# Routing and gather fed from the centred, weighted input, with factor and shift applied later, and token-on-partition variance sums

## The chip, the cores and the metric

One core of a Trainium2 chip runs the whole program in one launch. The metric is device time in microseconds, lower is better. TensorE is PE, VectorE is DVE, ScalarE is ACT, GpSimd is POOL, SyncE is SP.

## The reference, cut to what matters

Two transformer blocks run one after the other on x [1, 256, 1024], fp32. The second one is changed. Its two layers have a mixer (NSA, then MLA) and a mixture of 16 experts, each followed by a LayerNorm:

```python
def layer_norm(x, g, b):                 # LN_EPS = 1e-5
    mu = jnp.mean(xf, -1, keepdims=True)
    var = jnp.mean(jnp.square(xf - mu), -1, keepdims=True)
    y = (xf - mu) * lax.rsqrt(var + LN_EPS) * g + b
for i in range(2):
    ...                                  # y = mixer output @ w_out[i]
    x = layer_norm(DEEPNORM_ALPHA * x + y, ln_g[i, 0], ln_b[i, 0])
    f = hier_moe(x, ...)                 # 4 groups of 4 experts
    x = layer_norm(DEEPNORM_ALPHA * x + f, ln_g[i, 1], ln_b[i, 1])
# hier_moe: logits xs @ w_grp + b_grp (4) and xs @ w_exp + b_exp (16);
# best group, best 2 experts in it; sum of gate * (silu(x W_g) * (x W_u)) W_d
```

## The kernel before

x lies with features on partitions, as [128, 8, 256]: eight chunks of 128 features by 256 tokens. There are four LayerNorms (`LayerNorm`, L2033), numbered 0 to 3: 0 and 2 stand before the experts (the routing norms), 1 before MLA, 3 at the end. Each sums x over the features by ones times chunk on PE (L2062), centres on DVE (L2106), squares on ACT (L2083), sums the squares by ones times chunk on PE (L2068, 256 columns wide, the sum in every row), takes the square root of 128x256 on ACT (L2085) and the reciprocal on DVE (L2113), scales on DVE in four pieces (L2117), and applies gain g and shift b on ACT (L2093, six chunks) and DVE (L2121, two). `keep_busy` (its matmul is L323) issues matmuls on zeros, fillers. Norm 1 also carries `MemoryRows`: PE transposes of loaded memory rows (L2162), ACT copies of them (L2185), products (L2173).

The experts (`Moe`, L2749) start with routing. PE forms 20 logits a token from x (L2903) with a filler behind each chunk, and transposes x so that tokens lie on partitions (L2947), which ACT copies to `tok`. DVE finds the groups (from L3243), PE ranks the tokens (L2913 to L2915), DVE writes one-hot places (L3279 for slot 0, L3283 for the others), and PE gathers slot 0's tokens by them (L2960). ACT writes the rounded half x_hi (L3114), DVE the rest x_lo (L3312). Before the experts PE also transposes the one-hots (L2926), multiplies them with the gates (L2933), and each engine loads a plan (L2848), which says if a fifth slot of tokens is run.

Then run four expert groups of eight weight steps each, two a expert for gate and up, two for down. A step is 1 MB or 2 MB of weights from a ring that SP fills. ACT rounds a piece to w_hi (L3136, L3144), DVE forms w_lo (L3318, L3324), and PE does 24 matmuls of three products each step (L2964 to L2966). The order on every engine is the order in which each class's `pe`, `act` and `dve` issue; semaphores (`x_ready`, `ln_*`, `gu_hi`, `gu_lo`) and a PSUM bank plan connect them. `dve_first` (L3235) does the first weight pieces of step 0 inside the norm.

## Time and profile before

| | |
|---|---|
| Time, median of 3 runs | 2118.66 us (2119.27, 2115.07, 2118.66) |
| Profiled execution, its own time | 2114.99 us |
| Its span in the trace | 2113.2 us |
| Mean granted clock of PE | 0.996 |
| Busy share of PE, DVE, ACT, POOL | 97%, 69%, 53%, 1% |
| Weights and inputs read | 416.70 MB, 198 GB/s over the span |

PE is busy nearly all the time; the other engines have slack on average. The mean hides that in each routing stretch the engines work one after the other. These stretches are short, so they are read in the list of instructions by time, not in the shares. The granted clock is the share of the full 2.4 GHz that the chip gave PE: 1.00 is that level, 0.5 is 1.2 GHz.

### The profile page before, as it was taken

To read this page: it belongs to the slowest core of one execution; us is meant where nothing else is said; L and a number is where in the kernel's file an instruction comes from. 1 tells how busy PE (TensorE), PEld (TensorE's weight loads), DVE (VectorE), ACT (ScalarE), POOL (GpSimd) and SP (SyncE) were. 2 spreads that over 40 slices of the span, in tenths; PEclk is the share of its full clock that TensorE was granted. 3 is DMA by queue.
4 is the path that set the end of the run, shared out by engine and by line. 5 is a ranking of instruction groups with operands and counts; after the bars stand their busy time and mean duration, and the time that the engine had idled before them with its cause. 6 is when DMAs were issued, how large, how long until landed. Compare 5 with 4: busy or idle time off the path is not lost. (4 is left out here: it accounts for less than half of the span.)

```text
span 2113.2 us, 34585 instructions
## 1 busy us (share of the span) xinstructions
PE 2044.1 (97%) x14050; PEld 1853.5 (88%) x14050; DVE 1464.0 (69%) x2157; ACT 1114.7 (53%) x1580; POOL 26.3 (1%) x35
## 2 busy tenths in 40 slices
PE   7999999999999999989999989999999889999998
PEld 7999997999999998879999967888888758888886
DVE  5666785666666665576665477788987466888896
ACT  4333733544343445574333456677775455776774
POOL 1000000000000020000000000000000000000000
PEclk9999999999999999999999999999999999999999
DMA  9555322655545543435553532589985514789992
GB/s 310 186 186 184 123 89 92 211 185 186 186 148 185 185 146 100 154 124 189 186 184 124 156 123 100 204 323 368 351 328 207 220 40 160 271 328 337 343 359 93
DMA packets 246671, 421.44 MB, mean 199 GB/s; under 512 B 7716, under 2 KB 135104, under 8 KB 246432
## 3 DMA queue, kind: packets, MB, share of 16 engines
q1 hardware_dynamic: 245632, 418.09, 56.2%
q0 software_dynamic: 544, 1.62, 0.2%
q8 instruction: 73, 1.20, 0.2%
q10 hardware_dynamic: 384, 0.21, 0.1%
q14 instruction: 38, 0.31, 0.0%
HBM read 416.70 MB, written 1.05 MB: 198 GB/s over the span
## 5 line engine op out<-in xcount | busy, mean ns | idle before, releaser
L662 PE MATMUL banks<-x_hi,w_hi 128*128 128x256 f32 x1360 | 385.8, 284 | 0.0
L663 PE MATMUL banks<-x_lo,w_hi 128*128 128x256 f32 x1360 | 384.9, 283 | 0.0
L664 PE MATMUL banks<-x_hi,w_lo 128*128 128x256 f32 x1360 | 384.8, 283 | 0.0
L3318 DVE TENSOR_TENSOR w_lo<-weight_ring,w_hi 128x1024 fp32r<-128x1024 f32 x256 | 300.3, 1220 | 25.4 <-ACT w_hi L3136 16.9
L608 ACT ACTIVATE w_hi<-weight_ring 128x1024 fp32r<-128x1024 f32 x87 | 92.0, 1057 | 419.3 <-PE banks L664 419.2
L624 DVE TENSOR_TENSOR w_lo<-weight_ring,w_hi 128x1024 fp32r<-128x1024 f32 x88 | 107.7, 1224 | 242.4 <-ACT w_hi L608 242.4
L3136 ACT ACTIVATE w_hi<-weight_ring 128x1024 fp32r<-128x1024 f32 x256 | 256.0, 1053 | 36.0 <-PE banks L2966 20.4
L1084 DVE TENSOR_TENSOR pieces<-weight_ring,pieces 128x512 fp32r<-128x512 f32 (+2 forms) x245 | 167.8, 692 | 144.4 <-ACT pieces L1073 141.9
L662 PEld LDWEIGHTS banks<-x_hi,w_hi 128*128 128x128 f32 x1360 | 261.1, 192 | 0.2
L663 PEld LDWEIGHTS banks<-x_lo,w_hi 128*128 128x128 f32 x1360 | 261.1, 192 | 0.1
L664 PEld LDWEIGHTS banks<-x_hi,w_lo 128*128 128x128 f32 x1360 | 261.1, 192 | 0.0
L1018 PE MATMUL banks<-split,pieces 128*128 128x256 f32 (+2 forms) x824 | 239.6, 291 | 4.6 <-DVE split L451 2.6
L1073 ACT ACTIVATE pieces<-weight_ring 128x512 fp32r<-128x512 f32 (+2 forms) x245 | 151.9, 626 | 173.1 <-PE banks L1020 172.5
L1019 PE MATMUL banks<-split,pieces 128*128 128x256 f32 (+2 forms) x824 | 235.0, 285 | 0.0
L1020 PE MATMUL banks<-split,pieces 128*128 128x256 f32 (+2 forms) x824 | 234.8, 285 | 0.0
L615 DVE TENSOR_TENSOR w_lo<-weight_ring,w_hi 128x2048 fp32r<-128x2048 f32 x87 | 198.8, 2285 | 9.7 <-ACT w_hi L604 9.7
L2964 PE MATMUL banks<-w_hi,x_hi 128*128 128x512 f32 x512 | 202.9, 396 | 0.6 <-DVE w_lo L3318 0.6
L2966 PE MATMUL banks<-w_lo,x_hi 128*128 128x512 f32 x512 | 199.7, 390 | 0.0
L662 PE MATMUL banks<-h_hi,w_hi 128*128 128x256 f32 x704 | 199.5, 283 | 0.0
L2965 PE MATMUL banks<-w_hi,x_lo 128*128 128x512 f32 x512 | 199.3, 389 | 0.0
L663 PE MATMUL banks<-h_lo,w_hi 128*128 128x256 f32 x704 | 199.2, 283 | 0.0
L664 PE MATMUL banks<-h_hi,w_lo 128*128 128x256 f32 x704 | 199.2, 283 | 0.0
(406 smaller groups left out, 4079.8 us busy)
## 6 DMA issues: line engine op xcount, KB each, us to landing
weight_ring<-in_ffn_w_in SPq DMA_DIRECT2D x88, 1024.0 KB, 7.6
weight_ring<-in_moe_w_gate SPq DMA_DIRECT2D x64, 1024.0 KB, 6.6
weight_ring<-in_moe_w_up SPq DMA_DIRECT2D x64, 1024.0 KB, 9.0
weight_ring<-in_moe_w_down SPq DMA_DIRECT2D x48, 1024.0 KB, 11.9
weight_ring<-in_ffn_w_out SPq DMA_DIRECT2D x44, 1024.0 KB, 9.8
weight_ring<-in_moe_w_down SPq DMA_DIRECT2D x8, 2048.0 KB, 11.5
weight_ring<-in_hg_w_in SPq DMA_DIRECT2D x12, 1024.0 KB, 8.2
weight_ring<-in_fox_w_in SPq DMA_DIRECT2D x12, 1024.0 KB, 8.4
```

The source lines that it names most:

```text
L615: dve.tensor_tensor(k.w_lo[:, b, 0:2048].rearrange("p (k n) -> p k n", n=P), raw[:, 0:4096].rearrange("p (k n) -> p k n", n=256)[:, :, jj ...
L662: pe.matmul(out, w_hi, m_hi, start=start, stop=False, skip_group_check=True)
L663: pe.matmul(out, w_hi, m_lo, start=False, stop=False, skip_group_check=True)
L664: return pe.matmul(out, w_lo, m_hi, start=False, stop=stop, skip_group_check=True)
L1018: pe.matmul(out, l_hi, r_hi, start=start, stop=False, skip_group_check=True)
L1019: pe.matmul(out, l_hi, r_lo, start=False, stop=False, skip_group_check=True)
L1020: return pe.matmul(out, l_lo, r_hi, start=False, stop=stop, skip_group_check=True)
L2964: pe.matmul(out, m_hi, w_hi, start=start, stop=False, skip_group_check=True)
L2965: pe.matmul(out, m_lo, w_hi, start=False, stop=False, skip_group_check=True)
L2966: return pe.matmul(out, m_hi, w_lo, start=False, stop=stop, skip_group_check=True)
L3136: act.activation(self.gate_up_piece(s, p, self.w_hi), self.gate_up_piece(s, p), ACT.Copy).then_inc(sem["gu_hi"], 1)
L3318: dve.tensor_tensor(self.gate_up_piece(s, p, self.w_lo), self.gate_up_piece(s, p), self.gate_up_piece(s, p, self.w_hi.bitcast(F32)), ALU.s ...
```

## The change

In the routing norms, logits and transposes are taken from the centred x times g (`dve_gain`, `act_gain`). The factor 1/std is applied to the logits and in the copies to `tok`, the shift b in x_hi and x_lo (as bias), and b times the routing weights is added by eight 20-column matmuls. x itself, wanted again at the group's end, is scaled and shifted inside the first group (`dve_scale`, `act_shift`). In every norm the variance sums are matmuls of one column with the squares stationary, so std has a row for each token; where the factor is wanted along rows, a diagonal matrix times ones spreads it (`pe_rows`). In the routing norms DVE adds the first six chunks of x during the mixer (`dve_mean`). Place transposes, gates and the others' one-hots move into group 0, the plan's load into the last group. The fillers of the routing norms go, save four; the last norm has 12 for 17.

```diff
@@ -1213,6 +1215,8 @@
                 dve.wait_ge(k.x_ready, 4 * self.turn + done + 1)
                 k.banks.release(dve, f"{self.out_name}_o{done}")
+            if self.norm_after:
+                self.norm_after.dve_mean(dve, c)
@@ -2056,22 +2064,88 @@
         out = b.claim(pe, f"ln_m{i}")[:, 0:T]
+        if self.adds:
+            pe.wait_ge(k.ln_added, self.adds)
+            for kk in range(2):
+                pe.matmul(out, k.ones, k.sq[:, kk], start=kk == 0, stop=False)
+            pe.wait_ge(k.x_ready, 4 * self.before)
+            for kk in (KD - 2, KD - 1):
...
+        b.filled(last, f"ln_m{i}")
+        if self.routes is None:
+            self.sums_to = b.claim(pe, f"ln_v{i}")
+            for c in range(4):
+                last = self.pe_sums(pe, c)
+            b.filled(last, f"ln_v{i}")
+            self.pe_rows(pe)
+            if self.memory:
+                self.memory.pe_turned(pe)
+                self.memory.pe_products(pe)
+            else:
+                k.keep_busy(pe, k.psum[:, 0, :], 12)
+            return
...
-            last = pe.matmul(out, k.ones, k.x[:, kk], start=kk == 0, stop=kk == KD - 1)
...
-            last = pe.matmul(out, k.ones, k.sq[:, kk], start=kk == 0, stop=kk == KD - 1)
...
-        if not self.memory:
-            k.keep_busy(pe, k.psum[:, 0, :], 17)
...
+            last = pe.matmul(out, self.shift(kk).to_broadcast([P, P]), k.w_route[:, self.routes, kk], start=kk == 0, stop=kk == KD - 1)
+        b.filled(last, f"ln_c{i}")
+        self.sums_to = b.claim(pe, f"ln_v{i}")
+        self.logits_to = b.claim(pe, f"ln_lg{i}")
+        self.pe_sums(pe, 0)
+        self.pe_sums(pe, 1)
+        self.pe_logits(pe, 0)
+        self.pe_sums(pe, 2)
+        b.filled(self.pe_sums(pe, 3), f"ln_v{i}")
+        for c in (1, 2, 3):
+            last = self.pe_logits(pe, c)
+        b.filled(last, f"ln_lg{i}")
+    def pe_sums(self, pe, c):
+        k = self.k
+        pe.wait_ge(k.ln_sq, 4 * self.i + c + 1)
+        for kk in (2 * c, 2 * c + 1):
+            for t in range(TT):
+                last = pe.matmul(self.sums_to[:, t:t + 1], k.sq[:, kk, t * P:(t + 1) * P], k.ones[:, 0:1],
+                                 start=kk == 0 and t == 0, stop=kk == KD - 1, skip_group_check=True)
+        return last
+    def pe_logits(self, pe, c):
...
+        pe.wait_ge(k.ln_gained_dve if c < 2 else k.ln_gained_act, 2 * self.routes + c % 2 + 1)
+        for kk in (2 * c, 2 * c + 1):
+            for t in range(TT):
+                last = pe.matmul(self.logits_to[:, t * n:(t + 1) * n], k.x[:, kk, t * P:(t + 1) * P], k.w_route[:, self.routes, kk],
+                                 start=kk == 0 and t == 0, stop=kk == KD - 1, skip_group_check=True)
+        return last
+    def pe_rows(self, pe):
...
+        pe.wait_ge(k.ln_diag, 2 * self.i + 2)
+        for t in range(TT):
+            last = pe.matmul(out[:, t * P:(t + 1) * P], k.ones, self.diag[:, t * P:(t + 1) * P], start=True, stop=True, skip_group_check=True)
...
+    def act_shift(self, act, c):
...
+        act.activation(k.x[:, 2 * c], k.x[:, 2 * c], ACT.Identity, bias=self.shift(2 * c))
+        act.activation(k.x[:, 2 * c + 1], k.x[:, 2 * c + 1], ACT.Identity, bias=self.shift(2 * c + 1)).then_inc(k.x_ready, 1)
@@ -2081,17 +2155,59 @@
-        if self.memory:
-            act.wait_ge(k.x_ready, 4 * self.before)
-            self.memory.act_turned(act)
+        if self.routes is not None:
+            self.act_gain(act, 2)
+        src = b.wait(act, f"ln_v{i}")[:, 0:TT]
...
+        if self.routes is not None:
+            self.act_gain(act, 3)
+            return
         for c in range(3):
...
+        if self.memory:
+            act.wait_ge(k.x_ready, 4 * self.before)
+            self.memory.act_turned(act)
+    def act_gain(self, act, c):
...
+        act.activation(k.x[:, 2 * c], k.xn[:, 2 * c], ACT.Copy, scale=self.gain(2 * c))
+        act.activation(k.x[:, 2 * c + 1], k.xn[:, 2 * c + 1], ACT.Copy, scale=self.gain(2 * c + 1)).then_inc(k.ln_gained_act, 1)
+    def dve_gain(self, dve, c):
...
+        dve.tensor_scalar(k.x[:, 2 * c], k.xn[:, 2 * c], self.gain(2 * c), None, ALU.mult)
+        dve.tensor_scalar(k.x[:, 2 * c + 1], k.xn[:, 2 * c + 1], self.gain(2 * c + 1), None, ALU.mult).then_inc(k.ln_gained_dve, 1)
+    def dve_mean(self, dve, c):
...
+        if c == 1:
...
+            k.dve_seq.inc(dve.tensor_tensor(k.sq[:, 0:2], k.x[:, 0:2], k.x[:, 2:4], ALU.add))
...
+        if c == 2:
...
+            dve.tensor_tensor(k.sq[:, 0:2], k.sq[:, 0:2], k.x[:, 4:6], ALU.add).then_inc(k.ln_added, 1)
+            self.moe.dve_first(dve, (0,))
+    def dve_scale(self, dve, c):
...
+        dve.tensor_tensor(k.x[:, cs], k.x[:, cs], k.rstd[:].unsqueeze(1).to_broadcast([P, 2, T]), ALU.mult).then_inc(k.ln_scaled, 1)
+    def dve_rstd(self, dve):
...
+        k.banks.wait_read(dve, f"ln_v{i}")
+        dve.reciprocal(self.rstd_col, self.std_col).then_inc(k.ln_rstd, 1)
+        dve.wait_ge(k.ln_rstd, i + 1)
+        for t in range(TT):
+            dve.tensor_scalar(self.diag[:, t * P:(t + 1) * P], k.ident, self.rstd_col[:, t:t + 1], None, ALU.mult).then_inc(k.ln_diag, 1)
@@ -2107,19 +2223,26 @@
-        dve.reciprocal(k.rstd[:], k.std[:]).then_inc(k.ln_rstd, 1)
-        dve.wait_ge(k.ln_rstd, i + 1)
+        if self.routes is not None:
+            self.dve_gain(dve, 0)
+            self.dve_gain(dve, 1)
+            src, both = b.wait(dve, f"ln_c{i}")[:, 0:G_N + E_N], k.b_route[:, self.routes]
+            k.dve_seq.inc(dve.tensor_tensor(both, src, both, ALU.add))
+            k.dve_seq.wait(dve)
+            b.release(dve, f"ln_c{i}")
+            self.dve_rstd(dve)
+            return
+        self.dve_rstd(dve)
+        rstd = b.wait(dve, f"ln_r{i}")[:, 0:T].unsqueeze(1).to_broadcast([P, 2, T])
         for c in range(4):
             cs = slice(2 * c, 2 * c + 2)
-            dve.tensor_tensor(k.xn[:, cs], k.xn[:, cs], k.rstd[:].unsqueeze(1).to_broadcast([P, 2, T]), ALU.mult).then_inc(k.ln_scaled, 1)
+            dve.tensor_tensor(k.xn[:, cs], k.xn[:, cs], rstd, ALU.mult).then_inc(k.ln_scaled, 1)
...
+        b.release(dve, f"ln_r{i}")
         for kk in (KD - 2, KD - 1):
             g, bb = self.affine(kk)
             dve.tensor_scalar(k.x[:, kk], k.xn[:, kk], g, bb, ALU.mult, ALU.add).then_inc(k.ln_last, 1)
...
@@ -2894,18 +3021,11 @@
-        for kk in range(KD):
...
-                pe.wait_ge(k.x_ready, 4 * (self.turn - 1) + kk // 2 + 1)
-            for t in range(TT):
-                last = pe.matmul(out[:, t * 20:(t + 1) * 20], k.x[:, kk, t * P:(t + 1) * P], k.w_route[:, self.layer, kk],
...
-            k.keep_busy(pe, k.psum[:, 0, :], 1, 256)
-        b.filled(last, name + "lg")
...
-            self.pe_x_turned(pe, q)
+        self.pe_x_turned(pe, 0)
+        self.pe_x_turned(pe, 2)
+        self.norm.pe_rows(pe)
+        self.pe_x_turned(pe, 1)
+        self.pe_x_turned(pe, 3)
@@ -2913,30 +3033,45 @@
-        self.pe_x_turned(pe, 3)
         k.keep_busy(pe, k.psum[:, 0, :], 4, 256)
         pe.wait_ge(sem["placed"], 2 * self.layer + 2)
...
+    def pe_places(self, pe):
...
+        for i in range(self.SLOTS_N):
+            for t in range(TT):
+                last = pe.matmul(out[:, i * E_G:(i + 1) * E_G], self.place[:, t, i * P:(i + 1) * P], self.best[:, t], start=t == 0, stop=t == 1)
...
-        k.keep_busy(pe, k.psum[:, 0, :], 6)
...
-                last = pe.matmul(out[:, i * E_G:(i + 1) * E_G], self.place[:, t, i * P:(i + 1) * P], self.best[:, t], start=t == 0, stop=t == 1)
...
-        k.keep_busy(pe, k.psum[:, 0, :], 4)
-        count = self.load_plan(pe)
...
+    def act_places(self, act):
...
+        for q in range(3):
...
+            act.activation(self.place_t[:, q * 512:q * 512 + w], self.place_bank(q)[:, 0:w], ACT.Copy).then_inc(sem["places_read"], 1)
@@ -3037,6 +3172,9 @@
+            if s == 2 and i == 0:
+                self.pe_places(pe)
+                pe.wait_ge(sem["places_read"], 4 * self.layer + 4)
@@ -3085,22 +3223,20 @@
...
-            b.read(act.activation(self.tok[:, q // 2, (q % 2) * 512:(q % 2 + 1) * 512], src, ACT.Copy), f"{name}x{q}")
+            b.read(act.activation(self.tok[:, q // 2, (q % 2) * 512:(q % 2 + 1) * 512], src, ACT.Copy,
+                                  scale=self.norm.rstd_col[:, q // 2:q // 2 + 1]), f"{name}x{q}")
+            if q == 2:
+                src = b.wait(act, f"ln_r{self.norm.i}")[:, 0:T]
+                b.read(act.activation(k.rstd[:], src, ACT.Copy), f"ln_r{self.norm.i}")
...
         for c in range(2):
...
-            b.read(act.activation(self.place_t[:, q * 512:q * 512 + w], src[:, 0:w], ACT.Copy), f"{name}st{q}")
-        count = self.load_plan(act)
...
-        b.read(act.activation(self.gates[:, :, 0:E_G], src, ACT.Copy), name + "gates")
-        self.slots(act, count, self.act_slot, self.act_last_slot, self.act_skip)
+        self.slots(act, self.act_slot, self.act_last_slot, self.act_skip)
@@ -3111,8 +3247,9 @@
-        act.activation(self.x_hi[:, 4 * c:4 * c + 4], k.psum[:, 2 + c, :].rearrange("p (k n) -> p k n", n=P),
-                       ACT.Copy).then_inc(sem["xs_hi"], 1)
+        for n in range(4):
+            ins = act.activation(self.x_hi[:, 4 * c + n], k.psum[:, 2 + c, n * P:(n + 1) * P], ACT.Identity, bias=self.norm.shift(4 * c + n))
+        ins.then_inc(sem["xs_hi"], 1)
@@ -3189,7 +3326,11 @@
+                    if i == 0 and s == 2:
+                        self.act_places(act)
                 self.act_gate_up(act, s, p, self.step(i, s))
+            if i == 0 and s >= 4:
+                self.norm.act_shift(act, s - 4)
             if e:
@@ -3229,8 +3370,11 @@
-        count = self.load_plan(dve)
-        self.dve_slots(dve, count)
+        self.dve_tokens(dve, 0, 0)
+        self.dve_first(dve, (3,))
+        self.dve_tokens(dve, 0, 1)
+        self.dve_gates(dve)
+        self.dve_slots(dve)
@@ -3247,22 +3391,19 @@
...
+        lg = f"ln_lg{self.norm.i}"
+        src = b.wait(dve, lg)[:, 0:40].rearrange("p (t n) -> p t n", t=2)
+        for t in range(TT):
+            seq.inc(dve.scalar_tensor_tensor(out=self.logits[:, t], in0=src[:, t], scalar=self.norm.rstd_col[:, t:t + 1],
+                                             in1=k.b_route[:, self.layer], op0=ALU.mult, op1=ALU.add))
+        seq.wait(dve)
+        b.release(dve, lg)
@@ -3277,16 +3418,52 @@
+        do(dve.scalar_tensor_tensor(out=self.over, in0=src[0:1, 8:12], scalar=float(P), in1=k.const(C_LAST, 4, 1),
+                                    op0=ALU.is_gt, op1=ALU.mult))
+        b.release(dve, name + "rank")
+        self.dve_first(dve, (2,))
...
+    def dve_spread(self, dve):
...
         for t in range(TT):
             dve.tensor_tensor(self.place[:, t, P:6 * P].rearrange("p (i n) -> p i n", n=P),
...
+        do(dve.tensor_reduce(self.over[:, 0:1], self.over, X_AXIS, ALU.min))
+        do(dve.tensor_scalar(k.plan[:, 0:1], self.over[:, 0:1], 0.0, float(G_N), ALU.is_lt, ALU.add))
+        dve.tensor_scalar(k.plan[:, 1:2], self.over[:, 0:1], float(G_N), float(G_N - 1), ALU.add, ALU.min).then_inc(sem["planned"], 1)
+    def dve_gates(self, dve):
@@ -3299,18 +3476,15 @@
-        do(dve.tensor_reduce(self.over[:, 0:1], self.over, X_AXIS, ALU.min))
...
-        for c in range(2):
-            self.dve_tokens(dve, 0, c)
...
-                          self.x_hi[:, 4 * c:4 * c + 4].bitcast(F32), ALU.subtract).then_inc(sem["xs_lo"], 1)
+        for n in range(4):
+            ins = dve.scalar_tensor_tensor(out=self.x_lo[:, 4 * c + n], in0=k.psum[:, 2 + c, n * P:(n + 1) * P],
+                                           scalar=self.norm.shift(4 * c + n), in1=self.x_hi[:, 4 * c + n].bitcast(F32),
+                                           op0=ALU.add, op1=ALU.subtract)
+        ins.then_inc(sem["xs_lo"], 1)
     def dve_gate_up(self, dve, s, p, n):
@@ -3384,6 +3560,12 @@
+            if i == 0 and s == 1:
+                self.dve_spread(dve)
+            if i == 0 and 3 <= s < 7:
+                if s == 3:
+                    k.banks.wait_read(dve, f"ln_r{self.norm.i}")
+                self.norm.dve_scale(dve, s - 3)
```

PE, layer 0, between mean sums and routing. Before, the last variance sums and what follows (`squares`: x squared, `zeros`: filler, `x_res`: x):

```order
L2068 MATMUL banks<-squares,consts 128x256 [waits ln_sq]
L2068 MATMUL banks<-squares,consts 128x256
L323 MATMUL banks<-zeros 128x512 x17
L2903 MATMUL banks<-w_route,x_res 128x20 [waits x_ready,bank_free_0,small_ready]
L2903 MATMUL banks<-w_route,x_res 128x20
L323 MATMUL banks<-zeros 128x256
L2903 MATMUL banks<-w_route,x_res 128x20 x2
L323 MATMUL banks<-zeros 128x256
```

After, the same place:

```order
L2114 MATMUL banks<-consts,squares 128x1 [waits ln_sq,bank_free_1,bank_free_0]
L2114 MATMUL banks<-consts,squares 128x1 x3
L2114 MATMUL banks<-consts,squares 128x1 [waits ln_sq]
L2114 MATMUL banks<-consts,squares 128x1 x3
L2124 MATMUL banks<-w_route,x_res 128x20 [waits ln_gained_dve]
L2124 MATMUL banks<-w_route,x_res 128x20 x3
L2114 MATMUL banks<-consts,squares 128x1 [waits ln_sq]
```

The sums have one column, and logits stand between them without fillers.

DVE, layer 0, from the gates into the first weight steps. Before:

```order
L3302 TENSOR_REDUCE squares<-squares 1x1
L3303 TENSOR_SCALAR moe_plan<-squares 1x1 [waits dve_seq]
L3304 TENSOR_SCALAR moe_plan<-squares 1x1 [waits dve_seq]
L3312 TENSOR_TENSOR x_lo<-banks,x_hi 128x512 [waits moe_xs_hi] x2
L2848 TENSOR_LOAD moe_plan [waits moe_planned,bank_free_1]
L2848 ISA x2
L3318 TENSOR_TENSOR w_lo<-weight_ring,w_hi 128x1024 [waits moe_gu_hi] x4
L3318 TENSOR_TENSOR w_lo<-weight_ring,w_hi 128x1024 [waits moe_gu_lo,moe_gu_hi]
```

After (step 0's pieces, the other one-hots and the plan, then step 1's next pieces):

```order
L3478 TENSOR_TENSOR squares<-squares 128x8 [waits dve_seq]
L3492 TENSOR_TENSOR w_lo<-weight_ring,w_hi 128x1024 [waits moe_gu_hi] x4
L3446 TENSOR_REDUCE squares<-squares 128x2 [waits moe_gu_lo]
L3447 TENSOR_SCALAR squares<-squares 128x2 [waits dve_seq]
L3449 TENSOR_TENSOR wide<-consts,squares 128x640 [waits dve_seq]
L3449 TENSOR_TENSOR wide<-consts,squares 128x640
L3452 TENSOR_REDUCE squares<-squares 1x1
L3453 TENSOR_SCALAR moe_plan<-squares 1x1 [waits dve_seq]
L3454 TENSOR_SCALAR moe_plan<-squares 1x1 [waits dve_seq]
```

The gates and the one-hots for the other slots are now among weight pieces.

ACT in the norm before MLA. Before, from the square root on (`arena`: copies of memory rows):

```order
L2085 ACTIVATE std<-banks,consts 128x256 [waits bank_ready_3]
L2185 ACTIVATE arena<-banks 128x512 [waits bank_ready_0,x_ready]
L2185 ACTIVATE arena<-banks 128x512 [waits bank_ready_1]
L2185 ACTIVATE arena<-banks 128x512 [waits bank_ready_2]
L2185 ACTIVATE arena<-banks 128x512 [waits bank_ready_3]
L2093 ACTIVATE x_res<-wide,params 128x256 [waits ln_scaled]
```

After:

```order
L2169 ACTIVATE x_res<-wide,params 128x256
L2169 ACTIVATE x_res<-wide,params 128x256 [waits ln_scaled]
L2169 ACTIVATE x_res<-wide,params 128x256
L2308 ACTIVATE arena<-banks 128x512 [waits bank_ready_3,x_ready]
L2308 ACTIVATE arena<-banks 128x512 [waits bank_ready_0]
L2308 ACTIVATE arena<-banks 128x512 [waits bank_ready_1]
```

The memory copies now stand behind the six affine operations.

## Rows read from the trace of the kernel before

**Rows 1.** PE by time, layer 0: start, us, engine, line, tiles, shape, count [idle before].

```profile
1311.33 3.61 PE L2062 MATMUL banks<-x_res,consts 128*128 128x256 f32 x16
...
1320.00 3.83 PE L323 MATMUL banks<-zeros 128*128 128x512 bf16 x17
...
1325.01 0.52 PE L2903 MATMUL banks<-w_route,x_res 128*128 128x20 f32 x4
1325.37 0.27 PE L323 MATMUL banks<-zeros 128*128 128x256 bf16 x1
...
1327.88 0.89 PE L2903 MATMUL banks<-w_route,x_res 128*128 128x20 f32 x4
...
1328.77 2.67 PE L2947 MATMUL banks<-consts,x_res 128*128 128x128 f32 x12
...
1332.79 3.84 PE L2960 MATMUL banks<-wide 128*128 128x128 f32 x32
...
1338.85 2.29 PE L2933 MATMUL banks<-squares,wide 128*128 128x4 f32 x20
...
1341.71 0.55 PE L2964 MATMUL banks<-w_hi,x_hi 128*128 128x512 f32 x1
```

**Rows 2.** PE in order of time, layer 1.

```profile
1771.15 3.61 PE L2062 MATMUL banks<-x_res,consts 128*128 128x256 f32 x16
...
1788.15 1.47 PE L2947 MATMUL banks<-consts,x_res 128*128 128x128 f32 x12
```

**Rows 3.** ACT in order of time: the first SiLU of each expert layer.

```profile
1352.99 0.60 ACT L3150 ACTIVATE silu_gate<-banks 128x512 f32<-128x512 f32 x1 [1.66 <-PE banks L2966]
...
1811.38 0.60 ACT L3150 ACTIVATE silu_gate<-banks 128x512 f32<-128x512 f32 x1 [1.65 <-PE banks L2966]
```

**Rows 4.** busy by stretch, PE to POOL (instructions); last, granted clock and DMA share.

```profile
1324.40:1327.80 3.40, 3.34 (x35) 3.37 (x36) 1.40 (x4) 1.88 (x4) 0.00 (x0) 1.00 1.05 402
1327.80:1331.30 3.50, 3.50 (x20) 3.50 (x20) 1.82 (x11) 1.17 (x2) 0.00 (x0) 0.51 0.66 259
1357.00:1407.00 50.00, 50.00 (x236) 41.42 (x235) 44.30 (x42) 36.61 (x41) 0.00 (x0) 1.00 0.90 337
```

**Rows 5.** DVE in order of time, layer 0.

```profile
1312.36 2.36 DVE L3318 TENSOR_TENSOR w_lo<-weight_ring,w_hi 128x1024 fp32r<-128x1024 f32 x2
1314.98 2.48 DVE L2106 SCALAR_TENSOR_TENSOR wide<-banks,x_res 128x512 f32<-128x512 f32 x4 [0.26 <-PE banks L2062]
...
1320.71 1.75 DVE L2113 RECIPROCAL rstd<-std 128x256 f32<-128x256 f32 x1 [0.75 <-ACT std L2085]
1322.50 2.50 DVE L2117 TENSOR_TENSOR wide<-wide,rstd 128x512 f32<-128x512 f32 x4
1325.03 0.74 DVE L2121 TENSOR_SCALAR x_res<-wide,params 128x256 f32<-128x256 f32 x2
...
1333.04 1.56 DVE L3283 TENSOR_TENSOR wide<-consts,squares 128x640 f32<-128x640 f32 x2
...
1334.81 0.17 DVE L3252 TENSOR_TENSOR squares<-squares 128x8 f32<-128x8 f32 x1
...
1338.00 0.17 DVE L3301 TENSOR_TENSOR squares<-squares 128x8 f32<-128x8 f32 x1
```

**Rows 6.** ACT in order of time, layer 0.

```profile
1323.22 3.06 ACT L2093 ACTIVATE x_res<-wide,params 128x256 f32<-128x256 f32 x6 [2.55 <-DVE wide L2117]
...
1334.88 0.60 ACT L3114 ACTIVATE x_hi<-banks 128x512 fp32r<-128x512 f32 x1
```

**Rows 7.** ACT by form: shape, count | busy us, mean ns | idle before.

```profile
L1673 ACT ACTIVATE arena<-arena,att_cols 128x128 f32<-128x128 f32 x8 | 3.1, 386 | 0.0
```

**Rows 8.** PE and ACT in order of time, the norm before MLA.

```profile
1646.81 1.97 PE L2162 MATMUL banks<-consts,weight_ring 128*128 128x128 f32 x16 [3.39 <-DMA weight_ring<-in_mem_w_kv]
1649.89 5.42 PE L2173 MATMUL banks<-arena,weight_ring 128*128 128x256 f32 x24 [1.11 <-ACT arena L2185]
...
1647.57 2.06 ACT L2185 ACTIVATE arena<-banks 128x512 f32<-128x512 f32 x4 [3.63 <-PE banks L2162]
```

163 lines of the change are left out of this document (98 added, 65 removed).

## The prediction

> **What bounds the kernel now.** I read the page's busy shares first, then TensorE's order of time across one routing stretch, then the granted clock in short stretches. TensorE (PE) works nearly all the time, so only places where it does not do wanted work can give anything. The widest are the two stretches between a mixer's last matmul and the steady run of expert steps. In the first, the mean matmuls start at 1311.33 and the first expert matmul at 1341.71, which is 30.4 us; 17 fillers of 3.83 us lie in it, and the rest is matmuls that wait for VectorE (DVE) or ScalarE (ACT) one after the other [rows 1]. The second runs from 1771.15 [rows 2]. As a mark that stands in both kernels I take the start of weight step 2. It comes about 0.3 us before the first SiLU, so 41.4 us after the first mean matmul in layer 0 and 39.9 us in layer 1 (1352.99 and 1811.38) [rows 1, 2, 3]. From step 2 on PE is fed without a gap. The clock shows why the layers differ: it was 1.00 at 1324.40 to 1327.80, where PE was given 20-column matmuls with a filler behind every two, and 0.51, the lower level of 1.2 GHz, at 1327.80 to 1331.30 [rows 4]. Four 20-column records took 0.89 us there, 0.52 us before, and twelve transposes 2.67 us against 1.47 us in layer 1 [rows 1, 2].
>
> **The routing stretch, at the full clock.** All in us from the first mean matmul, t = 0.
> Mean: 16 records took 3.61 [rows 1], 0.225 each. Now two pieces (4 records, 0.9) run at once, two more when DVE has added the last part of x, and DVE has one weight piece before centring, not two (2.36 for two, 1.2 each) [rows 5]. Centring starts at 2.3, not 3.65. The two adds made for it and one weight piece (0.68 to 1.2) go among the mixer's last steps on DVE; a weight piece that ended late there would move x's last add, which I take as 0, at most 1.
> Centring takes 2.5 [rows 5], the first pair of gains 0.74 (the same form as the 0.74 pair at 1325.03) [rows 5]: 5.6. PE then has the first logits (8 records) and the last half of the sums (16 records). A narrow record costs 0.09 to 0.11 (the four at 1325.01 are followed by a filler at 1325.37; 20 in 2.29 at 1338.85) [rows 1], so 8.0. The square root of two columns 0.25, two gains of about 0.45 on ACT, last logits 0.7, end of pipeline 0.2: 10.1. The normalising of x (four at 0.62), the reciprocal of 256 columns (1.75) and the affine of 3.06 [rows 5, 6] have left the path. Sixteen transposes at 0.12 and four 128-column records bring 12.5; the rank, 0.8, and the two place columns, 0.7, bring 14.2 with DVE's grouping beside the transposes.
> Gather of one half: 16 of the 32 records in 3.84 [rows 1], 1.8. The copy to x_hi was one 0.60 [rows 6]; now it is four of 128 columns with a shift column. The nearest form is 386 ns [rows 7]; back to back I take 0.3, so 1.2. The Trainium skill (ScalarE: Activation LUTs, What ACT_TABLE_LOAD costs) gives 186 ns plus 0.833 ns a column plus some 93 ns for each pointer operand, with 93 ns overlap; by that, an estimate, the four take 1.27 us against 0.61 us for one, and the trace's 386 ns agrees with it. x_lo in four pieces is 0.9 to 1.1 for 0.68. So step 0 starts at 18.3, not 30.4 or 29.0: some 12 and 10.7 earlier.
>
> **What comes back.** The places, the gates and the plan were beside or in that stretch; they now stand in front of weight pieces on DVE. After step 0's data DVE has a weight piece 1.2, four x_lo 1.1, seventeen gate operations 3.36 (1334.81 to the one at 1338.00) [rows 5] and then the first piece of step 1, 1.2: 6.9, against 5.5 that step 0 takes PE (24 records at 0.228). PE stops 1.4. Three more pieces and the spread (0.4 and twice 0.78 [rows 5]) end 12.4 after the start of step 0. PE then does 20 narrow records, 2.2 [rows 1], ten transposes, 1.2, and waits 0.7 for ACT's last copy before step 2. That is 16.5 from step 0 to step 2 where it was 10.9. Step 2 starts at 34.8: 6.6 earlier in layer 0, 5.1 in layer 1.
> Later in the group DVE gets four scalings of 0.62 and ACT eight shifts of about 0.5. DVE was busy 44.30 of 50 us there and PE never waited [rows 4], so the 2.5 fits into 5.7; 0 to 1 a layer, I take 0.1. The plan is loaded in the last group instead: sequencer work of under 1 us that PE's queue can cover, 0 to 0.8, I take 0.15 a layer. SyncE's order is untouched; its refill of the first ring slot waits for a weight piece that is now 11 us later, still over 10 us before it is wanted. Together 0.5.
>
> **The two plain norms.** The sums become narrow, the reciprocal falls from 1.75 [rows 5] to 0.2, but two diagonals (0.55) and a product with a read through PSUM (0.7) come in: about 1.2 earlier at the scaling. Before MLA that gains nothing, because PE waits 3.39 for the memory weights [rows 8]. ACT now does the six affine operations, 3.06, ahead of the four memory copies (1647.57, products from 1649.89) [rows 8]. They end some 1.0 later, so +1.0 (0.3 to 2). At the very end the 1.2 counts: -1.1.
> At the full clock: -6.6 - 5.1 + 1.0 - 1.1 + 0.5 = -11.3.
>
> **The clock decides.** The change takes away the 17 fillers and the eight behind the logits. From 1.9, the end of the mean, to 10.1 PE would have nothing but one- and 20-column records and pauses, less than what stood before the fall at 1327.80, where it still had fillers. I therefore expect the clock at 1.2 GHz from about 5 to 7 until the transposes and the gather are well under way. Priced by the rows at that level, four narrow records took 0.37 more and twelve transposes 1.2 more [rows 1, 2], so 0.18 for 0.09 and 0.21 for 0.12 a record: the first logits and late sums add 2.1, the last three logits, which lose ACT's cover, 2.2, transposes and rank 2.3, less 1.5 for the part after the clock is back. Sum 5.1. Then step 2 starts at 39.9: 1.5 earlier in layer 0, 0 in layer 1. In the norm before MLA the memory transposes and the first products would fall into the lower clock: +2.0 in all (1 to 5). In the last norm the fillers and transposes: +0.2 in all. Total -1.5 + 0 + 2.0 + 0.2 + 0.5 = +1.2.
> The Trainium skill (TensorE: Matmul & The Clock Gate, Back-to-back issue gap) puts 1 to 64 columns at about 60 cycles, 25 ns. By that, an estimate, the 16 narrow records after the first logits would take 0.4 us rather than the 1.5 that my price makes of them; the trace has 0.09 or more a record, with a weight load each, and speaks for the row.
>
> **Rivals.** Full clock (A): -11.3. For it: layer 1 kept the clock through the same logits; against: it had the fillers. One layer only keeps it (B): -6.
> Slower (C): the lower clock lasts into the expert steps. The place is the stop of step 2, with 20 narrow records, the wait of 0.7 and the stall before step 1; with a second such fall of 3.4 us in each layer, 1.7 is lost in each, and with 1.7 more in each of the two norms it is 6.8 above the forecast. It decides as soon as PE is at the lower level behind its first 20 expert records.
> The spread work is not hidden (D): if DVE has no room at all in the first group, the 2.5 of scalings and 2.2 of x_lo, plan and waits come on the path in each layer, +9 over the forecast. DVE's 5.7 idle speaks against it.
>
> **How the numbers follow.** The profiled run is 2114.99, its span 2113.2; the median of the runs is 2118.66, and they lie 4 us apart. The forecast is 2114.99 + 1.2 = 2116.2 in the profile's terms and 2119.9 added to the median. Some of the median's distance may be falls of the clock that I have already counted in the changed kernel, so I say 2118.0. A is 2107.4, B 2113, C 2125, D 2127. Chances: forecast 0.55, A 0.16, B 0.11, C 0.14, D 0.04. The forecast's own range, with the ends named above, is 2112 to 2124. From A to a little short of C holds 8 in 10: 2107 to 2124. A measurement tells 0.2%, 4.2 us, from no change. A, most of B and a seventh of the forecast are faster: 0.32. C, D and an eighth of the forecast are slower: 0.25. The rest is 0.43.
>
> **What would show it.** Right: step 0 7 to 8 us earlier after the first mean matmul (near 23), the clock near 0.5 over several us of the logits and transposes, the 20-column records at 0.18 each; step 1 late by about 1.4 on a weight piece; 4 us between steps 1 and 2. Wrong: the clock 1.00 from mean to gather, then step 0 near 18 and A. If step 0 is near 18 and the total does not move, the gain was given back in the first group (D).

## The result, and the profile after

The changed kernel takes 2134.46 us, median of 5 runs (2132.43 to 2140.19), against 2118.79 for the kernel before (5 runs). The ratio is 1.0079, 95% interval 1.0064 to 1.0093: slower by 0.8%, some 16 us. I had said 2118.0, within 2107 to 2124. The profiled execution took 2135.26 us, its span 2133.3 against 2113.2. Of the executions of the kernels below one, of e4_before_nofill, took 7487.10 us at a granted clock of 1.00; it is left out of the figures.

The first lines of the page after: the span, then the busy time of each engine.

```profile
span 2133.3 us, 34754 instructions
## 1 busy us (share of the span) xinstructions
PE 2061.3 (97%) x14062; PEld 1874.3 (88%) x14071; DVE 1469.7 (69%) x2225; ACT 1127.7 (53%) x1642; POOL 26.3 (1%) x35
```

PE is busy 17.2 us longer than before with almost the same number of matmuls, and the mean granted clock is 0.981 where it was 0.996. So the first thing to look for is the lower clock. Busy time by stretch of the kernel after (columns as in [rows 4]); these are the four norms:

```profile
1321.20:1334.90 13.70, 13.70 (x67) 13.70 (x67) 3.41 (x20) 4.92 (x10) 0.00 (x0) 0.51 0.15 58
1792.30:1802.60 10.30, 10.30 (x51) 10.30 (x52) 2.65 (x16) 3.22 (x7) 0.00 (x0) 0.52 0.04 14
1649.50:1659.70 10.20, 8.97 (x42) 8.48 (x41) 3.76 (x9) 4.36 (x9) 0.00 (x0) 0.51 1.03 398
2117.30:2127.60 10.30, 8.92 (x32) 5.91 (x34) 3.86 (x9) 3.96 (x8) 0.00 (x0) 0.52 0.00 0
```

The clock is at 1.2 GHz for 13.7 and 10.3 us in the routing norms, and for 10 us in each plain norm, where the profile of before shows no fall in its plain norms and one of 3.4 us in a routing norm [rows 4]. The plain norms of before:

```profile
1634.50:1660.00 25.50, 19.46 (x95) 16.57 (x96) 11.77 (x18) 12.80 (x23) 0.00 (x0) 1.00 0.81 309
2092.00:2107.50 15.50, 11.34 (x52) 7.87 (x53) 7.73 (x12) 7.24 (x12) 0.00 (x0) 1.00 0.00 1
```

PE in order of time across the routing stretch of layer 0 of the kernel after:

```profile
1315.91 1.02 PE L2070 MATMUL banks<-squares,consts 128*128 128x256 f32 x4
...
1319.58 1.92 PE L2114 MATMUL banks<-consts,squares 128*128 128x1 f32 x16
...
1322.94 3.55 PE L2114 MATMUL banks<-consts,squares 128*128 128x1 f32 x16
1326.36 5.29 PE L2124 MATMUL banks<-w_route,x_res 128*128 128x20 f32 x24
1331.48 1.95 PE L3082 MATMUL banks<-consts,x_res 128*128 128x128 f32 x8
...
1341.63 0.47 PE L3099 MATMUL banks<-w_hi,x_hi 128*128 128x512 f32 x1 [0.76 <-issue]
...
1348.37 0.47 PE L3099 MATMUL banks<-w_hi,x_hi 128*128 128x512 f32 x1 [1.05 <-DVE w_lo L3492]
...
1354.23 2.37 PE L3056 MATMUL banks<-squares,wide 128*128 128x4 f32 x20
1356.46 1.29 PE L3062 MATMUL banks<-consts,wide 128*128 128x128 f32 x10
1358.54 0.50 PE L3099 MATMUL banks<-w_hi,x_hi 128*128 128x512 f32 x1 [0.80 <-ACT place_t L3074]
```

A record is one matmul entry of the trace (an fp32 matmul has two); a narrow one has a single or 20 columns. The first 16 one-column sums take 1.9 us, 0.12 each with the pipeline's end; from 1322.94 on a narrow record takes 0.21, from start to start (16 in 3.42, then 24 in 5.12). Step 0 starts 25.7 us after the mixer's end (30.4 in [rows 1]), step 1 is 1.3 late on a weight piece, and gates, places and a wait for ACT take 4.3 us (1354.23 to 1358.54) between steps 1 and 2. I call this last place the stop of step 2. Step 2 comes 42.6 us after the first mean matmul, and 40.7 in layer 1, where it was 41.4 and 39.9 before: 1.2 and 0.8 later.

The intervals below are all differences of starts in the lists by time, in us. A: start of the first mean matmul of the first routing norm, the first block and the NSA mixer run before it, alike in all but two additions and one weight piece on DVE in the mixer's last steps. B: from the first mean matmul of a routing norm to step 0 (layer 0, layer 1). C: from the same start to the second SiLU, so C less B is the time from step 0 to the second SiLU. D: second SiLU to the next norm's first mean matmul, the expert groups. E: norm 1 to the end of the MLA mixer. F: last norm to the transposes of the output. "Again" is a second profile of the same kernel.

| Kernel | A | B | C | D | E | F | span |
|---|---|---|---|---|---|---|---|
| before | 1311.3 | 30.4, 28.9 | 55.9, 54.4 | 267.3, 266.5 | 136.7 | 15.1 | 2113.2 |
| before again | 1316.3 | 33.5, 28.9 | 59.0, 54.5 | 268.4, 266.6 | 138.9 | 15.1 | 2124.8 |
| after | 1315.9 | 25.7, 24.1 | 57.1, 55.1 | 269.9, 269.4 | 142.4 | 17.6 | 2133.3 |
| after again | 1316.0 | 25.7, 25.7 | 57.1, 56.7 | 270.0, 269.4 | 140.7 | 17.5 | 2133.3 |
| e1_fill | 1312.7 | 29.5, 27.8 | 60.8, 58.8 | 271.9, 269.4 | 144.2 | 18.0 | 2141.6 |
| e2_one_shift | 1313.5 | 24.8, 24.7 | 56.7, 58.0 | 267.3, 267.1 | 140.7 | 15.9 | 2125.2 |
| e3_plain | 1313.6 | 26.9, 27.3 | 59.8, 58.3 | 269.9, 269.6 | 140.8 | 15.1 | 2133.1 |
| e4_before_nofill | 1313.6 | 33.4, 35.5 | 58.9, 61.0 | 266.6, 266.5 | 141.0 | 15.1 | 2128.6 |
| e5_before_pieces | 1314.3 | 30.3, 28.9 | 55.9, 54.4 | 270.2, 268.7 | 133.3 | 15.1 | 2118.5 |
| e6_dense | 1315.1 | 25.0, 25.0 | 59.0, 57.3 | 270.0, 269.3 | 138.5 | 15.9 | 2131.2 |
| e7_tok | 1313.0 | 25.7, 24.1 | 59.7, 55.1 | 267.2, 267.2 | 140.0 | 15.1 | 2123.5 |
| v2_dense_forms | 1315.2 | 21.8, 21.8 | 54.0, 52.7 | 267.3, 267.3 | 138.3 | 15.1 | 2116.1 |
| v3_places | 1316.5 | 23.4, 21.8 | 52.0, 50.4 | 267.3, 267.3 | 136.0 | 15.1 | 2111.2 |
| e8_before_fill1 | 1312.8 | 30.4, 29.0 | 55.9, 54.5 | 267.3, 266.5 | 136.2 | 15.1 | 2114.3 |

The first two rows warn how far one profile can be trusted. The same kernel showed 2113.2 and 2124.8, and the difference lies wherever the clock fell: A moved by 5.0 us in unchanged code, B of layer 0 by 3.1, E by 2.2. In its second profile the kernel before, with all its fillers, is at the lower clock for 10.3 us of the routing stretch of layer 0:

```profile
1332.30:1342.60 10.30, 10.30 (x53) 10.05 (x54) 5.87 (x29) 3.98 (x7) 0.00 (x0) 0.50 0.28 109
```

The page on which I predicted was an execution with few falls. Averaged over two profiles each, after minus before is: A +2.1, C -0.4 and +1.4, D +2.1 and +2.8, E +3.8, F +2.4, together +14.2. So by the second SiLU the routing stretch gives nothing, and D, E and F, which I had at +2.6 in all, cost 11. Two profiles of each are few: only D and F repeat closely enough in both kernels (within 1.1 us) to be read to a microsecond.

### The profile page after: what moved, and what is told of

The parts are those of the page before. It is cut to its first block, busy times and chain, and to the rows that moved or that the text cites. A ratio compares the mean times of both kernels' runs of the same rounds, so it can differ in the third digit from the quotient of the medians.

```text
span 2133.3 us, 34754 instructions
## 1 busy us (share of the span) xinstructions
PE 2061.3 (97%) x14062; PEld 1874.3 (88%) x14071; DVE 1469.7 (69%) x2225; ACT 1127.7 (53%) x1642; POOL 26.3 (1%) x35
## 4 chain that ended last, share of the span: by engine, by line
PE 88%; DVE 5%; ACT 4%; DMA 1%; issue 1%; ACTq 0%; DVEq 0%; SPq 0%; PEldq 0%
PE banks L664 11%; PE banks L666 11%; PE banks L665 11%; PE banks L3099 8%; PE banks L3101 8%; PE banks L3100 8%; PE banks L1020 5%; PE banks L1022 5%; PE banks L1021 5%; PE banks L3095 1%; PE banks L2114 1%; PE banks L1307 1%; DMA weight_ring<-in_ffn_w_out 1%; DVE w_lo L3492 1%; PE banks L2296 1%
## 5 line engine op out<-in xcount | busy, mean ns | idle before, releaser
L3492 DVE TENSOR_TENSOR w_lo<-weight_ring,w_hi 128x1024 fp32r<-128x1024 f32 x256 | 299.9, 1219 | 15.3 <-ACT w_hi L3273 7.2
```

The costliest lines, as they stand in the source:

```text
L3492: dve.tensor_tensor(self.gate_up_piece(s, p, self.w_lo), self.gate_up_piece(s, p), self.gate_up_piece(s, p, self.w_hi.bitcast(F32)), ALU.s ...
```

## The experiments

### Two suspects: the clock and the four pieces

The expert groups (D) are slower by 2 to 3 us a layer, long after the routing. PE's waits there, before (1384 to 1634) and after (1390 to 1643): engine and line that waited, on what, us in total, times, longest.

```profile
PE banks L2964 <- DVE w_lo L3318: 0.3, 2, 0.2
```
```profile
PE banks L3099 <- DVE w_lo L3492: 2.4, 3, 0.8
PE banks L3209 <- DVE x_lo L3484: 1.0, 1, 1.0
```

w_lo (L3492 on DVE) is late by 2.4 us in three waits, one at each border between groups, and x_lo itself once by 1.0. DVE in order of time at the first border, before and then after, with PE's first matmul that waits below each:

```profile
1413.67 0.69 DVE L3312 TENSOR_TENSOR x_lo<-banks,x_hi 128x512 fp32r<-128x512 f32 x1 [0.33 <-ACT x_hi L3114]
...
1415.90 0.50 PE L2964 MATMUL banks<-w_hi,x_hi 128*128 128x512 f32 x1 [0.16 <-DVE w_lo L3318]
```
```profile
1419.98 1.13 DVE L3484 SCALAR_TENSOR_TENSOR x_lo<-banks,params,x_hi 128x128 fp32r<-128x128 f32 x4 [0.45 <-ACT x_hi L3251]
...
1422.30 0.50 PE L3099 MATMUL banks<-w_hi,x_hi 128*128 128x512 f32 x1 [0.79 <-DVE w_lo L3492]
```

The four operations for x_lo take 1.13 us where one took 0.69, and DVE waits 0.45 for x_hi instead of 0.33. `act_tokens` and `dve_tokens` serve every gather, not only that of slot 0, and at a border DVE has no slack: PE waits 0.79 for the piece behind instead of 0.16.

**e1_fill.** One filler in each gap between narrow records of the routing norms:

```diff
             for t in range(TT):
                 last = pe.matmul(...)
+            if self.routes is not None and kk < KD - 1:
+                k.keep_busy(pe, k.psum[:, 0, :], 1)
```

> The changed kernel with one 512-column filler behind every two or four narrow records of the routing norms (19 to 20 fillers a layer, 0.22 us each). Theory 'clock': the lower clock makes the narrow records 0.21 us instead of 0.11, so with the clock held the time from the mixer's end to weight step 2 falls from 42.6 and 41.0 us to 36 to 38, in all 8 to 10 us less than the changed kernel's 2134.5: near 2125. Rival 'pieces' (the loss lies in the expert groups, not in the norms): the fillers only add PE work, 2134 to 2142.

Measured: 2135.64 us (6 runs, 2125.91 to 2147.27), ratio 1.0073 (1.0044 to 1.0101). This lies in the rival's range, but doesn't decide between the two: the clock wasn't held. It fell all the same and stayed down 17 us, and the spread is the widest of all:

```profile
1319.00:1336.00 17.00, 17.00 (x80) 16.02 (x79) 2.66 (x16) 4.46 (x8) 0.00 (x0) 0.50 0.05 21
```
```profile
1317.18 0.38 PE L325 MATMUL banks<-zeros 128*128 128x512 bf16 x1
...
1322.17 0.59 PE L325 MATMUL banks<-zeros 128*128 128x512 bf16 x1
```

A filler shows 0.38 us at 1.00 and 0.59 at 0.50, so thin fillers that don't hold the clock only lengthen the stretch: B is 29.5 and 27.8, against 25.7 and 24.1. D of layer 0 is 2.0 longer too, but not in the groups: the mean matmuls of norm 1 wait 2.85 for PE's sequencer, 0.90 in the changed kernel.

**e2_one_shift.** One operation each for x_hi and x_lo; the shift b is then missing from the experts' input, which changes values and not the amount of work:

```diff
-        for n in range(4):
-            ins = act.activation(self.x_hi[:, 4 * c + n], ..., ACT.Identity, bias=self.norm.shift(4 * c + n))
+        act.activation(self.x_hi[:, 4 * c:4 * c + 4], k.psum[:, 2 + c, :]..., ACT.Copy).then_inc(sem["xs_hi"], 1)
```

> The changed kernel with x_hi and x_lo formed by one operation of 512 columns, as before, in place of four of 128; the shift b is left out of the experts' input. Theory 'pieces': DVE has 0.43 and ACT 0.54 us less at each of the eight gathers a layer, w_lo of the next group is no longer late, and the time from the second SiLU to the next norm falls from 269.9 and 269.4 to the 267.3 and 266.5 of the kernel before; with 1 us a layer ahead of step 0 that is 7 us less: 2127. Rival 'scalings' (the late w_lo come from the scalings and shifts of x in the first group): the later group boundaries keep their 0.6 to 1.0 us and the total falls by 2 at most.

Measured: 2127.47 us (6 runs, to 2131.28), ratio 1.0043 (1.0030 to 1.0056). D is back at 267.3 and 267.1. The theory 'pieces' holds: the total falls by 7.0 us, of which D is 4.9. The scalings and shifts in the first group are cleared: they are still in this kernel.

**e3_plain.** The two plain norms as before (256-column sums, memory copies ahead of the affine, 17 fillers at the end).

> The changed kernel with the two plain norms (1 and 3) as they were before: 256-column sums, memory copies ahead of the affine operations, 17 fillers in the last. Theory 'narrow sums lower the clock in the plain norms too': norm 1 to the end of the MLA mixer falls from 142.4 to 136.7 us and norm 3 to the end's transposes from 17.6 to 15.1: 8 us less, 2126. Rival 'only the order of the copies counts': the clock still falls at the same places and 1 to 2 us come back.

Measured: 2134.18 us (6 runs), ratio 1.0067 (1.0054 to 1.0079). Half right. F falls from 17.6 to 15.1 as forecast. E doesn't fall to 136.7: the clock drops in norm 1 here too. And B grew by 1.2 and 3.2 us though nothing in the routing norms was changed. The low stretches there were 17 us each, as against 13.7 and 10.3. So the total shows no gain, and the 2.4 us of F are read from the profile alone. In F, too, the time goes with the clock: the changed last norm, which took 17.6, took 15.9 in e2 and in e6, where the clock was down for 6.8 us and not 10.2.

**e4_before_nofill.** The kernel before, without 17 + 8 fillers a routing norm:

```diff
-        if not self.memory:
+        if self.i == 3:
             k.keep_busy(pe, k.psum[:, 0, :], 17)
...
-            k.keep_busy(pe, k.psum[:, 0, :], 1, 256)
```

> The kernel before without the 17 fillers behind the sums of the routing norms and the eight behind the logits. Theory 'clock': the clock is at the lower level over logits and transposes in both layers, and each layer takes 2 to 4 us longer to step 0: 2122 to 2127. Rival 'the fillers only fill waits': 2118 to 2119, no change, or 1 us less a layer since eight fillers stood between the logits.

Measured: 2131.80 us (5 runs), ratio 1.0058 (1.0044 to 1.0073). The clock theory holds, and its size is larger than I gave it. B is 3.0 and 6.5 us longer than in the first profile of before (in layer 0 no longer than in before again), and the clock in the two stretches:

```profile
1326.00:1337.00 11.00, 10.26 (x49) 10.29 (x50) 3.90 (x17) 4.36 (x9) 0.00 (x0) 0.53 0.58 226
1791.00:1808.00 17.00, 14.87 (x71) 14.65 (x72) 8.91 (x34) 7.04 (x13) 0.00 (x0) 0.50 0.47 179
```

So in the kernel before these fillers, which compute nothing, were worth some 12.3 us (2131.80 against 2119.51 in the same comparison). B has 9.5 of it at most. In this profile E, whose code is unchanged, is 2 to 4 us longer than in the two of before; whether the missing fillers brought that about isn't shown. The change also takes out ten fillers a layer (6 and 4) beside the places and gates, which this kernel keeps and my prediction left out; what they are worth wasn't tested.

### What each is worth alone

**e5_before_pieces.** The kernel before with the four pieces at each gather, nothing else (the shift is then added twice).

> The kernel before with one part of the change alone: x_hi and x_lo in four operations of 128 columns with a shift column at each gather (the shift is added although x has it already, so the experts' input is off). Theory 'pieces': the time from the second SiLU to the next norm rises from 267.3 and 266.5 us to 269.9 and 269.4, and step 0 starts 1 us later in each layer: 2126 against 2119. Rival 'the pieces cost only together with the scalings, gates and places that the change put into the group': under 2 us, 2119 to 2121.

Measured: 2121.52 us (12 runs), ratio 1.0019 (1.0005 to 1.0034): 3.4 us by the medians, between the two, and the interval, 1 to 7 us, reaches both. D decides. It rises by 2.9 and 2.2, as theory 'pieces' has it. Ahead of step 0 the pieces cost nothing (B unchanged), where I had 1 us a layer. In this profile E is 133.3, 3.4 less than before, because PE's wait of 3.39 us for the memory weights [rows 8] is gone: norm 1 started later against that transfer, and its mean took 5.41 us at the lower clock:

```profile
1640.27 5.41 PE L2062 MATMUL banks<-x_res,consts 128*128 128x256 f32 x16 [2.20 <-issue]
...
1650.78 1.97 PE L2162 MATMUL banks<-consts,weight_ring 128*128 128x128 f32 x16
```

Part of a loss ahead of a wait on a transfer is given back in the wait. That it explains the whole of the small total isn't shown, since one profile carries it.

**e6_dense.** Two fillers a gap instead of one.

> The changed kernel with two 512-column fillers (0.43 us) in each of the gaps in which the kernel with one filler had one. Theory 'clock': the array is now busy enough, the clock stays at 1.00 from the mean to the gather, narrow records take 0.11 us, and step 0 starts near 25 to 27 us after the mixer's end in spite of 8.6 us of fillers, where one filler a gap gave 29.5 and 27.8; the total is 2128 to 2134, with a smaller spread over the runs. Rival 'fillers of this kind don't hold it': step 0 at 33 or later, the total over 2140.

Measured: 2132.75 us (6 runs, 2132.14 to 2136.65), ratio 1.0066 (1.0051 to 1.0082). As the clock theory has it in the routing stretch: 1.00 from mean to gather, and a spread of 4.5 us where one filler gave 21.4.

```profile
1316.00:1340.00 24.00, 22.94 (x181) 19.85 (x181) 10.75 (x36) 11.69 (x25) 0.00 (x0) 1.00 0.27 105
```
```profile
1321.38 0.50 PE L2116 MATMUL banks<-consts,squares 128*128 128x1 f32 x4
1321.74 0.59 PE L325 MATMUL banks<-zeros 128*128 128x512 bf16 x2
...
1331.69 1.07 PE L3088 MATMUL banks<-consts,x_res 128*128 128x128 f32 x8
...
1340.02 0.47 PE L3105 MATMUL banks<-w_hi,x_hi 128*128 128x512 f32 x1 [0.76 <-issue]
```

Four narrow records now take 0.36 us (1321.38 to 1321.74), 0.09 each. But the 34 fillers are 7.3 us of PE's time, and step 0 comes at 25.0 in both layers, where low clock and no fillers gave 25.7 and 24.1. From the fillers' own time I get what the changed kernel would do with the clock free: 1.9 for the mean, 80 records at 0.093 (7.5), and 8.3 from the first transpose to step 0, so at least 17.7.

But here the clock fell later. From step 0 to the second SiLU e6_dense takes 34.1 and 32.4 us, the changed kernel 31.3 and 31.0. PE's clock right behind the stop of step 2 in layer 0, first of this kernel, then of e7_tok (next):

```profile
1356.10:1362.70 6.60, 5.80 (x16) 4.50 (x16) 3.50 (x3) 3.61 (x6) 0.00 (x0) 0.50 0.72 275
```
```profile
1353.40:1360.10 6.70, 6.17 (x22) 4.99 (x23) 3.92 (x5) 4.49 (x7) 0.00 (x0) 0.51 0.86 333
```

This is the place that rival C named. The clock falls there in e2 and e6 (both layers), and in layer 0 of e3, e7 and v2, and it doesn't in either profile of the changed kernel, nor in e1 and v3. From step 0 to the second SiLU a layer takes 31.0 to 31.3 us where it doesn't fall (28.6 in v3, which has a shorter stop), and 31.9 to 34.1 where it does: 1 to 3 us. That holding the clock ahead of step 0 brings on the later fall isn't shown; e3 and e7 have both.

**e7_tok.** The whole of the layer's work, but without most of the pieces: the shift is added once to `tok`, on DVE in group 0, and slot 0 alone keeps the four pieces; plain norms as before.

```diff
+                piece = self.tok[:, t, h * 512:(h + 1) * 512]
+                dve.tensor_tensor(piece, piece, self.b_rows[:, h * 512:(h + 1) * 512], ALU.add).then_inc(k.tok_shifted, 1)
-            if i == 0 and 3 <= s < 7:
+            if i == 1 and 3 <= s < 7:
```

> The changed kernel with x_hi and x_lo in one operation again from the second gather on (the shift b is added to the transposed tokens once, on DVE in group 0; the scalings and shifts of x move to group 1), and with the two plain norms as before. Theory 'pieces': the groups fall back to 267.3 and 266.5 us, 5.5 us in all, and the last norm to 15.1 from 17.6: 2126 to 2127. Rival 'DVE is short of time in group 0 whatever it does there': the four additions of 0.69 take back 2 us a layer, 2130.

Measured: 2125.97 us (12 runs), ratio 1.0034 (1.0024 to 1.0044). D 267.2 and 267.2, F 15.1: as 'pieces' has it, and the four additions in group 0 are hidden. C of layer 0 is 2.6 longer than in the changed kernel, with the same B: that is the fall behind the stop of step 2, shown above.

### Keeping the clock with wanted work

**v2_dense_forms.** e7_tok with wide matmuls for sums and logits:

```diff
-            for t in range(TT):
-                last = pe.matmul(self.sums_to[:, t:t + 1], k.sq[:, kk, t * P:(t + 1) * P], k.ones[:, 0:1], ...)
+            last = pe.matmul(self.sums_to, k.ones, k.sq[:, kk], start=kk == 0, stop=kk == KD - 1)
...
-            for t in range(TT):
-                last = pe.matmul(self.logits_to[:, t * n:(t + 1) * n], k.x[:, kk, t * P:(t + 1) * P], k.w_route[...], ...)
+            last = pe.matmul(self.logits_to, k.w_route[:, self.routes, kk], k.x[:, kk], start=kk == 0, stop=kk == KD - 1)
...
+            pe.matmul(out[:, 40 + t:41 + t], k.std[:, t * P:(t + 1) * P], k.ident[:, 0:1], ...)
+            last = pe.matmul(out[:, t * 20:(t + 1) * 20], k.sq[:, KD - 1, t * P:(t + 1) * P], k.ident[:, 0:20], ...)
```

> The kernel of e7_tok with wide forms in the routing norms: sums as ones times squares (16 records of 256 columns, 0.225 us each, against 32 of one column), logits with the routing weights stationary and x moving (16 records of 256 columns against 32 of 20), then two turned products that bring logits and std to tokens on partitions; no fillers. Theory 'clock': PE is dense from the mean to the gather, the clock stays at 1.00, step 0 starts 17 to 20 us after the mixer's end (30.4 and 28.9 in the kernel before), step 2 by 33.5 to 36.5: 2110 to 2115, faster than both kernels. Rival 'the chain of ACT and DVE sets it': step 0 at 22 or later with the clock at 1.00, 2117 to 2121.

Measured: 2118.73 us (12 runs), ratio to before 1.0005 (0.9993 to 1.0017). PE in layer 0 (sums, sums, the last logits, step 0), and its clock over the stretch:

```profile
1318.85 1.97 PE L2115 MATMUL banks<-squares,consts 128*128 128x256 f32 x8
...
1321.72 1.99 PE L2115 MATMUL banks<-squares,consts 128*128 128x256 f32 x8
1323.64 2.77 PE L2126 MATMUL banks<-x_res,w_route 128*20 128x256 f32 x12
...
1336.94 0.47 PE L3111 MATMUL banks<-w_hi,x_hi 128*128 128x512 f32 x1 [0.77 <-issue]
```
```profile
1315.20:1336.90 21.70, 19.70 (x128) 15.24 (x126) 11.77 (x39) 11.76 (x25) 0.53 (x1) 1.00 0.40 155
```

The clock is 1.00 with four fillers left, and B is 21.8 in both layers: 8.6 and 7.2 less than before, 4.0 and 2.3 less than the changed kernel. The wide sums cost PE about what the narrow ones do at the full clock (16 in 3.9 us here; 32 at 0.093 to 0.12 are 3.0 to 3.8). But by the second SiLU only 1.8 and 1.7 of it are left: both theories had a part, and in layer 0 some 1.3 more went to a fall of 3.4 us behind the stop of step 2 (32.3 us from step 0 to the second SiLU, 31.0 in layer 1).

**v3_places.** v2 with the first eleven gate operations on DVE ahead of x_lo, the places turned before the gates are multiplied, the copies waited for where the bank is wanted, and 14 fillers ahead of norm 1's memory transposes:

```diff
+        self.dve_best(dve)
         self.dve_tokens(dve, 0, 0)
...
-                pe.wait_ge(sem["places_read"], 4 * self.layer + 4)
+                pe.wait_ge(sem["places_read"], 4 * self.layer + 2)
...
+                k.keep_busy(pe, k.psum[:, 0, :], 14)
                 self.memory.pe_turned(pe)
```

> The kernel of v2_dense_forms with the first half of the gate operations on DVE ahead of x_lo (DVE idled 2.2 us there), the places turned before the gates are multiplied and their copies waited for only where the bank is wanted, and 14 fillers of 512 columns (3.1 us) ahead of the memory transposes in norm 1. Theory 'the first group gives the gain back by the stop ahead of step 2 and the late pieces of step 1': from step 0 to the second SiLU it takes 29 to 30 us where it took 32.3 and 31.0, 2 to 3 us less a layer, and norm 1 to the end of the MLA mixer takes 136 to 137 instead of 138.3: 2112 to 2115, faster than both kernels. Rival 'the stop is PE's own work': under 1 us a layer, 2117.

Measured: 2110.92 us (5 runs, 2109.12 to 2113.00), ratio to before 0.9956 (0.9942 to 0.9969): faster than both. From step 0 to the second SiLU 28.6 us in both layers (v2: 32.3 and 31.0; after: 31.3 and 31.0). The clock didn't fall behind the stop here, so of the 3.7 us in layer 0 only some 2.4, as in layer 1, are the new order's. Wide forms don't hold the clock each time: here it fell for 3.4 us in the routing stretch of layer 0, and B is 23.4 there, 21.8 in layer 1. The stop ahead of step 2:

```profile
1350.84 1.03 PE L3076 MATMUL banks<-consts,wide 128*128 128x128 f32 x8
1351.71 2.29 PE L3071 MATMUL banks<-squares,wide 128*128 128x4 f32 x20
...
1354.04 0.48 PE L3114 MATMUL banks<-w_hi,x_hi 128*128 128x512 f32 x1
```

PE goes from the turned places and the gates' product into step 2 without the 0.80 that it waited for ACT after 1356.46 in the changed kernel. The kernel differs from v2 in four things, and only the fillers in norm 1 were measured alone (next).

**e8_before_fill1.** The kernel before with only those 14 fillers in norm 1.

> The kernel before with 14 fillers of 512 columns (3.1 us) ahead of the memory transposes in norm 1, where PE waits some 3.4 us for the memory weights. Theory 'that wait brings the clock down in most executions' (138 to 141 us from norm 1 to the end of the MLA mixer in kernels whose norm 1 is the same, 136.7 in the one profile of before): the interval stays at 136 to 137 and the median falls by 2 to 3 us, to 2115.5. Rival 'the fall is not from that wait': no change, 2118.

Measured: 2115.88 us (11 runs), ratio 0.9983 (0.9973 to 0.9994): 0.17%, some 3.6 us, at the edge of what can be told. PE in norm 1, first of before again, then of this kernel:

```profile
1655.61 2.75 PE L2162 MATMUL banks<-consts,weight_ring 128*128 128x128 f32 x16 [2.96 <-DMA weight_ring<-in_mem_w_kv]
1659.27 9.21 PE L2173 MATMUL banks<-arena,weight_ring 128*128 128x256 f32 x32 [0.92 <-ACT arena L2185]
```
```profile
1644.81 3.19 PE L323 MATMUL banks<-zeros 128*128 128x512 bf16 x14
1648.03 1.96 PE L2163 MATMUL banks<-consts,weight_ring 128*128 128x128 f32 x16
1651.10 7.14 PE L2174 MATMUL banks<-arena,weight_ring 128*128 128x256 f32 x32 [1.11 <-ACT arena L2186]
```

Without fillers the wait of 2.96 us is followed by transposes of 2.75 and products of 9.21; with them 1.96 and 7.14. But the first profile of before had 1.97 after a wait of 3.39 [rows 8], and products of 7.14, without these fillers. What speaks for the theory is the count: with them neither profile (this one, v3) has a fall in norm 1; without them the wait was 3.0 to 4.1 us in before, before again, e3, e4, e7 and v2, and five of these six fell.

**before_again and after_again.**

> The kernel before, one more profile. If the first profile was an execution with few falls of the clock (granted 0.996, where other executions show 0.988 to 0.996), this one shows 10 to 20 us more at the lower clock, norm 1 to the MLA mixer's end near 139 to 141 us, and a time of 2116 to 2121. If not, the intervals repeat within 0.3 us.

Measured: 2126.58 us, granted clock 0.988. The direction is as expected, the size above the range I gave. D's 1.1 us more in layer 0 are small parts: PE waits 0.8 instead of 0.3 for w_lo, and 1.9 instead of 1.7 for the last x ahead of norm 1; the rest I can't place.

> The changed kernel, one more profile. The expert groups (269.9 and 269.4 us from the second SiLU to the next norm) repeat within 0.3 us if they are set by DVE and not by the clock; the routing stretches, norm 1 and the last norm move by up to 3 us either way with where the clock falls, and the first mean starts at 1311 to 1316.

Measured: 2135.20 us, span 2133.3. D repeats within 0.1 us; layer 1's B is 1.6 longer. The changed kernel's five executions showed granted clocks of 0.978 to 0.983, those of before 0.988 to 0.996: its falls come nearly every time.

## Why the prediction was wrong

**The mechanism was right.** I had said that the clock falls in both routing stretches once the fillers are gone, and eats the gain. It did; e4 shows it in the kernel before, e6 and v2 the other way round. Near 23 us to step 0 was forecast, 25.7 came. But the sum built on it failed. Against the averages of two profiles each it is short by 4.4 us in the groups (D), 3.3 in the last norm (F), some 2.5 from the routing norms to the second SiLU (C), and 0.8 in norm 1 to the end of MLA (E); 2.1 more lie ahead of the first routing norm (A), in nearly unchanged code, and moved by 5.0 between two profiles of one kernel.

**The step that failed first: the four pieces.** The largest missing term was one that I put at nothing. In the part on the routing stretch I costed x_hi and x_lo for slot 0 (1.2 and some 1.0 us), and "What comes back" has for the rest of the groups only scalings, shifts and plan, 0.5 us. The same two functions serve all gathers. Measured 2.7 and 2.9 us in D against the first profile, taken back by e2 and e7 to within 0.8; without the pieces the total fell by 7.0 us. I read which line changed and not who calls it. And I called DVE's idle 5.7 of 50 us room; at a group's border there is none.

**The size of the lower clock.** My price for a narrow record there was 0.18 us; it is 0.213, and the row that I took it from already said 0.22 (four in 0.89 [rows 1]). I subtracted 0.52, which is how long the four at the full clock lasted with the pipeline's end, where from start to start they took 0.36 (1325.01 to 1325.37). The stretch lasted 13.7 and 10.3 us, so the term of 5.1 was about 7.4 in layer 0 and 5.8 in layer 1 (25.7 and 24.1 against my 18.3 at the full clock, which e6's at least 17.7 leaves standing). Step 2, forecast at 39.9, came at 42.6 and 40.7.

**The plain norms.** I had +2.0 for the clock in norm 1, +0.2 in the last and -1.1 gained there. In the last norm it came to +2.4 instead of -0.9. PE after:

```profile
2114.99 5.22 PE L2114 MATMUL banks<-consts,squares 128*128 128x1 f32 x32 [1.54 <-ACT squares L2157]
...
2122.79 4.69 PE L325 MATMUL banks<-zeros 128*128 128x512 bf16 x11 [0.22 <-issue]
2127.32 1.91 PE L923 MATMUL banks<-consts,x_res 128*128 128x128 f32 x16
```

32 one-column records take 5.2 us, against 3.7 for 16 wide ones, and the fillers (11 of the 12 are in the trace) 4.7 us at the lower clock. e3 shows the term by taking it back: 15.1. In norm 1 the forecast was +3.0 in all, and E rose by 5.8 against the first profile, 3.8 between the averages. PE after:

```profile
1648.13 5.91 PE L2114 MATMUL banks<-consts,squares 128*128 128x1 f32 x32 [1.54 <-ACT squares L2157]
...
1662.40 8.83 PE L2296 MATMUL banks<-arena,weight_ring 128*128 128x256 f32 x32 [2.49 <-ACT arena L2308]
```

The sums and the spread of the factor swallow the wait for the memory weights, and the products then wait 2.49 for ACT's copies, 1.38 more than the 1.11 of [rows 8]: the +1.0 for their new place was about right. How much of the rest is the change's isn't settled, since the unchanged norm 1 of e4, e7 and before again falls to the lower clock too.

**What held.** Step 0 to step 2 was forecast at 16.5 us, and is 16.9 (1341.63 to 1358.54); step 1 late by 1.4, and is by 1.3; scalings, shifts and the plan's load hidden (e2, where D is within 0.6 us of before).

**The base.** The forecast stood on a profile with few falls, 2114.99. I saw that the median lay 3.7 us above it and took part of that off, where I should have doubted the profile: a second one of before differed by 11.6 us. Of the rivals D (2127) came nearest in number, and DVE without room was right in kind; but it blamed the scalings and the rest of the first group, which e2 clears, and it had no pieces at the later gathers. Rival C (2125) named the right place for a later fall, the stop of step 2, but the changed kernel is not among those that fell there.

**The two rules.** The Trainium skill (ScalarE: Activation LUTs, What ACT_TABLE_LOAD costs) made four copies for x_hi 1.27 us; the profile after has 1.14 for four (1.2 was my own term), so it agrees within 0.13. The Trainium skill (TensorE: Matmul & The Clock Gate, Back-to-back issue gap) gave a matmul of 1 to 64 columns some 25 ns; at the full clock e6 has 0.09 us a record, each with a weight load of 128 columns, so it doesn't price these.

## What to carry to other kernels

Before fillers or wide matmuls are replaced by narrow ones, count PE's time at the lower clock for the whole stretch and for what follows: a narrow form that saves arithmetic saved no time here (at the full clock 32 records of one column took what 16 of 256 take), and it gave up the clock. When the clock is held in one stretch, read the next stop too: in e6 it fell there, and that cost 2.8 and 1.4 us. For each changed line ask who else calls it, and price it where the engine has no slack. Where the clock falls in some executions, one profile is one draw: compare intervals of two.

## What was unexpected of the hardware

The lower clock lasted. The one fall in the routing norms of before's first profile is 3.4 us, but in stretches of thin work it stayed down 10 to 17 us (10.3 in before again too), and one filler a gap did not shorten it (17 in e1). Two a gap held it (e6), but cost as much as they saved. A wait of 3 to 4 us for a transfer stood ahead of a fall in norm 1 in five of six profiles, and with 14 fillers in that wait the kernel before was some 3.6 us faster, an effect whose interval (0.6 to 5.7) nearly reaches nothing.
